# Hybrid decoder trunk on Trainium2: eight experts written out straight in the first pass, in place of a loop over pairs

## What is computed

```python
def moe_swiglu(h, router, w_in, w_out):
    t = h.reshape(b * s, d)                       # 256 x 1024
    logits = (t @ router).astype(jnp.float32)
    top_vals, top_idx = lax.top_k(logits, TOP_K)  # 2 of 8
    gates = jax.nn.softmax(top_vals, axis=-1)
    combine = jnp.sum(jax.nn.one_hot(top_idx, N_EXPERTS, dtype=jnp.float32) * gates[..., None], axis=1)
    for e in range(N_EXPERTS):
        y = y + combine[:, e:e + 1] * swiglu(t, w_in[e], w_out[e])
```

## Time and profile before

| | |
|---|---|
| median of 3 runs | 1569.99 us (1569.7 to 1570.82) |
| the profiled execution | 1570.96 us, its span 1569.2 us |
| instructions in the trace | 21897 |
| DMA | 426.88 MB, mean 272 GB/s |
| mean granted TensorE clock | 0.986 |

### The profile page before, as it was taken

The page is one execution under the profiler, slowest core; times in us unless marked ns, Lnnn a source line. Parts: engine busy times, 40 slices in busy tenths (PEclk is TensorE's granted clock), DMA queues, the critical chain, the costliest instruction groups (busy, mean ns, idle before and its releaser), DMA issues.

```text
span 1569.2 us, 21897 instructions
## 1 busy us (share of the span) xinstructions
PE 1513.6 (96%) x8223; PEld 1276.2 (81%) x8223; DVE 1199.7 (76%) x1033; ACT 994.5 (63%) x855; POOL 127.1 (8%) x192
## 2 busy tenths in 40 slices
PE   6999999999999699999999999999998999999998
PEld 6967999989997478888888877888887888888886
DVE  6966544565485768888888888888987888888887
ACT  5657433465545567776776676677776677677774
POOL 8900000000152300000000000000000000000000
PEclk9979999999999899999999999999999999999999
DMA  9503655546500369999999999999998999999994
GB/s 302 188 1 120 210 183 186 186 149 200 184 32 21 127 242 368 336 366 341 348 360 345 348 340 335 355 346 360 354 341 323 340 347 364 347 343 366 346 364 163
DMA packets 205346, 426.88 MB, mean 272 GB/s; under 512 B 6737, under 2 KB 56074, under 8 KB 205242
## 3 DMA queue, kind: packets, MB, share of 16 engines
q1 hardware_dynamic: 204880, 424.78, 76.6%
q0 software_dynamic: 320, 0.69, 0.2%
q10 hardware_dynamic: 42, 0.01, 0.0%
HBM read 424.41 MB, written 1.05 MB: 271 GB/s over the span
## 4 chain that ended last, share of the span: by engine, by line
PE 68%; DVE 2%; ACT 1%; issue 1%; DVEq 0%; ACTq 0%
PE bank L1287 20%; PE bank L1288 20%; PE bank L1289 20%; PE bank L1541 2%; PE bank L1647 2%; PE bank L1618 1%; DVE w_l L275 1%; PE bank L1523 0%; PE bank L1522 0%; PE bank L1631 0%; PE bank L1630 0%; ACT w_h L270 0%; PE bank L1554 0%; DVE h_l L511 0%; PE bank L1564 0%
## 5 line engine op out<-in xcount | busy, mean ns | idle before, releaser
L275 DVE TENSOR_TENSOR w_l<-raw,w_h 128x2048 fp32r<-128x2048 f32 x403 | 922.0, 2291 | 259.1 <-ACT w_h L270 258.1
L270 ACT ACTIVATE w_h<-raw 128x2048 fp32r<-128x2048 f32 x403 | 772.8, 1918 | 404.3 <-PE bank L1289 402.3
L1287 PE MATMUL bank<-w_h,hs_h 128*128 128x512 f32 x896 | 359.5, 401 | 6.5 <-issue 2.6
L1288 PE MATMUL bank<-w_l,hs_h 128*128 128x512 f32 x896 | 353.5, 395 | 3.7 <-issue 3.7
L1289 PE MATMUL bank<-w_h,hs_l 128*128 128x512 f32 x896 | 353.8, 395 | 0.0
L1287 PEld LDWEIGHTS bank<-w_h,hs_h 128*128 128x128 f32 x896 | 168.1, 188 | 45.2 <-issue 3.0
L1289 PEld LDWEIGHTS bank<-w_h,hs_l 128*128 128x128 f32 x896 | 168.0, 187 | 44.9 <-issue 4.1
L1287 PE MATMUL bank<-h_h,w_h 128*128 128x256 f32 x672 | 193.0, 287 | 6.3 <-DVE h_l L511 6.3
L1288 PEld LDWEIGHTS bank<-w_l,hs_h 128*128 128x128 f32 x896 | 168.3, 188 | 37.9
L1288 PE MATMUL bank<-h_l,w_h 128*128 128x256 f32 x672 | 191.1, 284 | 0.0
L1289 PE MATMUL bank<-h_h,w_l 128*128 128x256 f32 x672 | 191.0, 284 | 0.0
(11 more groups left out here) (275 smaller groups left out, 1413.0 us busy)
## 6 DMA issues: line engine op xcount, KB each, us to landing
raw<-in_moe_w_in SPq DMA_DIRECT2D x224, 1024.0 KB, 5.7
raw<-in_moe_w_out SPq DMA_DIRECT2D x112, 1024.0 KB, 5.5
raw<-in_ffn_w_in SPq DMA_DIRECT2D x22, 1024.0 KB, 5.1
raw<-in_hgrn_w_in SPq DMA_DIRECT2D x16, 1024.0 KB, 5.5
raw<-in_ffn_w_out SPq DMA_DIRECT2D x11, 1024.0 KB, 4.9
raw<-in_ab_w_in SPq DMA_DIRECT2D x10, 1024.0 KB, 11.7
raw<-in_ab_w_out SPq DMA_DIRECT2D x4, 1024.0 KB, 5.0
raw<-in_hgrn_w_out SPq DMA_DIRECT2D x4, 1024.0 KB, 4.9
```

Of the source, the lines that this page charges most:

```text
L270: act.activation(w_h[:, u0 % S, :], raw[:, u0 % R, :], ACT.Copy).then_inc(w_high, 1)
L275: eng.tensor_tensor(w_l[:, u0 % S, :], raw[:, u0 % R, :], w_h[:, u0 % S, :], ALU.subtract).then_inc(w_low, 1)
L1287: pe.matmul(o, a_high, b_high, start=start, stop=False, skip_group_check=True)
L1288: pe.matmul(o, a_high, b_low, start=False, stop=False, skip_group_check=True)
```

## The change

In the first pass (r = 0) `moe_experts` writes out all eight experts one after the other, with numbers known at build time, and returns. The second pass keeps the loop. An expert's slots in the rings, its buffers and the order of its steps are those of before.

```diff
+            if r == 0:
+                for e in range(NE):
+                    expert(e, e, 0, e % 2, e == NE - 1)
+                return
             expert(0, 0, 0, 0, False)
             with fori(0, (NE - 2) // 2) as pair:
                 for h in range(2):
```

## The result

The changed kernel takes **1561.49 us** (1561.39 to 1561.7, 4 runs) against 1570.4 us (1569.7 to 1572.36, 4 runs) for the kernel before: ratio 0.9941, 95% interval 0.9924 to 0.9959. It is faster by 8.9 us; 1560.3 was forecast, and the range was 1558.6 to 1564.4. The profiled execution took 1561.39 us with a span of 1559.4, 9.8 us less than the 1569.2 of before.

A forecast was written before the change was run, and what follows sets the result against it. TensorE was taken as the bound, waiting for its instructions after two jumps back in the expert loop. Removing them gives -9.65 us, all other parts 0: 1560.3 us against the median 1569.99, range 1558.6 to 1564.4.

The forecast's parts named there:

- the 8.8 us of idle time: TensorE's idle gaps at the expert loop's two jumps back, summed: 2.58 + 1.86 + 2.48 + 1.84 us.
- Parts 2, 4, 5: Expert loop: entering and leaving it, ScalarE's and VectorE's short jumps, and addresses and wait values made constants; gain 0 each.
- part 5: Addresses and wait values in the expert loop become constants; gain 0, bounds -0.3 and +0.3 us.
- Part 3: SyncE's jump in the expert loop stops load issue for 5.7 us; nothing waits, gain 0, but the cover grows.
- Part 6: Experts 1 to 6 written out add code to fetch; cost per block taken as 0, bounds 0 and 1.86 us.
- rival C: TensorE outruns its straight code in experts 1 to 6; 56 us added, 1616 us; chance 0.03.
- the second gap: TensorE idle 1.86 us, thirteen matmuls and four transposes after the first gap at a jump back; read as awaiting the second block.
- Rival A: Hand-over gaps aren't the branch's: VectorE's subtraction holds TensorE (1564.1) or the second gap stays (1564.4); chance 0.04 together.
- the 5.6 us of this case: Only the first stall at each expert-loop jump goes, the second stays: 2.83 + 2.73 = 5.6 us gained.
- the other half of A: TensorE waits for VectorE's w_l subtraction at the jumps; only 5.9 us go, 1564.1; chance 0.04 with the second-gap case.
- Rival B: No change: loads become the expert stage's bound, 9.65 us turn up as ScalarE waiting for raw; 1570; chance 0.02.
- The reading of the dense loop: Dense layer's loop branch takes 0.2 us without a gap; its body has 242 matmuls against 1182 in a pair of experts.

The follow-up runs named there:

- the run of one turn: Changed kernel, but experts 1 to 6 sit in a loop of a single turn on all four engines, never jumping back; 1561.65 us, ratio 0.9940.
- The two shifts: Kernel before plus unneeded small matmuls ahead of the expert stage: 24 (48 instructions) 1568.17 us, ratio 0.9978; 15 (30 instructions) 1579.04 us, ratio 1.0046.
- the run with 2299 instructions: Changed kernel with TensorE's dense loop in 2 turns of 4 steps, plus 165 unneeded matmuls a step; 1635.32 us, one run.
- a body of 1645 instructions: Changed kernel with TensorE's dense loop in 2 turns of 4 steps, plus 83 unneeded matmuls a step; 1597.83 us, one run.

## Why the prediction was right, and where it wasn't

**The bound and the sum.** TensorE, with only its own code to wait for, and 9.65 us by the difference of the stretches: measured 9.55 in the trace, 8.9 in the median. Taking stretches rather than the 8.8 us of idle time was right by the trace. Between 8.8 and 9.6 the timed runs can't decide.

**Parts 2, 4, 5.** The entry and the exit cost nothing: the run of one turn has both and takes 125.29 to 125.32 us a stretch. The registers cost nothing either, by the reason that part 5 gave, the looped stretches without a jump; the run that was meant to test it had no register work left. ScalarE's and VectorE's jumps are free: with SyncE alone straight the loss is what it is with all three.

**Part 3, SyncE's jump, is the step that was wrong in its reason.** "Nothing waits: gain 0" looked only at who waits for the loads. True as to them: with TensorE straight, SyncE's jump costs nothing. But while TensorE jumps too, SyncE's jump is half of the price: 9.6 us for both, 4.6 to 4.9 for TensorE's alone, 0 for SyncE's alone. What was missed is that a pause in issuing is followed by a pile of loads, and that TensorE's blocks travel with them. The sum didn't suffer, since the change took away both; that is luck of this change. The same reason gave 0 for the run with the other three engines straight, and it gained 4.9 us.

**Part 6 and rival C.** Straight code costs nothing: no idle TensorE in six experts, 61 blocks on the larger instruction queue instead of 67. The prediction rightly took the second gap for the second block, but not why it came late: the target stood near the end of its own block, and thirteen matmuls and four transposes were too little work for the 6 us until the next block's packet. The two shifts show that. In straight code TensorE works through whole blocks, some 25 us each, and TensorE never stood for one, which is what C would have needed.

**Rival A** gave "the second gap belongs to the code and not to the jump" a chance. It does hang on the code's place (shifted away by 48 instructions, made 2.7 us longer by 30), yet without the jump there is none, so that the 5.6 us of this case fell short of the 9.55 measured. The chain of waits and the named releaser, w_l, spoke for the other half of A, and were wrong.

**Rival B** fell as forecast: 352 GB/s in each stretch, and loads that land in 5.8 and 5.4 us.

**The reading of the dense loop** (free because its body is short) was right in kind; the run with 2299 instructions shows it away from the expert stage and its full DMA queues. The two-page window that the Trainium skill gives (Runtime: NRT & Kernel Launch, Instruction fetch mechanics) is not what decides for TensorE: a body of 1645 instructions is held. The 2048 instructions that the same section of the Trainium skill gives as the size for PE lie between the two measured bodies; no run here comes nearer to it.

## What to carry to other kernels

A loop on TensorE cost nothing while its body was still held (1645 instructions were, 2299 weren't); beyond, a jump back cost the first fetch less what was queued, and the second fetch less the work left in the target's block. The other engines' bodies weren't varied: with 259 and 272 recorded instructions of a pair, ScalarE and VectorE jump in 0.05 and 0.06 us, and SyncE, with 338, is away for 5.7 us. Look for the duration of the branch instruction and for idle time put down to issue, cut the span at a repeated instruction, and compare stretches with a jump to those without. Write out straight the engine that is the bound; a pause in the issue of loads on another engine can lengthen its fetch without ever making it wait for data.

## What was not expected

Fifteen unneeded matmuls in idle time made the kernel 8 us slower, and twenty-four made it some 3 us faster, by the place where the loop's code begins and, in the slower one, the clock behind the longer gap. An edit to TensorE's code ahead of a loop too long to be held can thus move the time, in either direction, without touching the loop.

An idle piece of 4.59 us, three matmuls after one of 2.70, went with a granted clock of 0.50 for 6.8 us, and so did 4.51 us after 2.62 at the second jump; 2.58 and 1.86 us with thirteen matmuls between did not. Whether the long piece alone would do it, no run shows.
